# One weight block of the experts in the place of channel-major x, with x made anew from its token-major copy at the first scatter

## What is computed

```python
for l in range(DEPTH):
    xn = rms_norm(x, norm_mix[l])
    c_q, c_kv, k_rope, dq, dk, dv, mu, mv, mo, mg = jnp.split(xn @ w_in[l], split_at, axis=-1)
    ...
    x = x + jnp.concatenate([y_mla, y_dil, y_ml], axis=-1) @ w_out[l]
    x = x + hier_moe(rms_norm(x, norm_ffn[l]), ...)        # 16 experts
# hier_moe: h = silu(x @ w_gate) * (x @ w_up) * weight_of_token ; y = h @ w_down
```

## Time and profile before

| | |
|---|---|
| median of 3 runs | 1823.51 us (1822.35 to 1825.17) |
| the profiled execution | 1822.44 us |
| its span, first to last instruction | 1820.7 us |
| PE busy, of the span | 1776.5 us (98%) |
| DVE / ACT busy | 741.8 us (41%) / 309.2 us (17%) |
| moved by DMA | 546.86 MB, mean 300 GB/s |
| expert stage of layer 0 / layer 1, first expert product to the last scatter | about 462 to 915 us / 1367 to 1817 us |

### The profile page before, as it was taken

One profiled execution on the slowest core, in us unless ns is written; L12 is line 12 of the kernel. 1 busy time (PEld: TensorE's weight loads), 2 busy tenths in 40 slices (PEclk: granted clock), 3 DMA queues, 4 the chain that ended last, 5 costly groups with the idle time before them and its releaser, 6 DMA issues.

```text
span 1820.7 us, 27290 instructions
## 1 busy us (share of the span) xinstructions
PE 1776.5 (98%) x11754; PEld 1338.8 (74%) x11754; DVE 741.8 (41%) x1563; ACT 309.2 (17%) x830; POOL 13.8 (1%) x27
## 2 busy tenths in 40 slices
PE   9999999999999999899999999999999999999898
PEld 9788888899665566655597888878995755657555
DVE  3477665676302212012225775656762111121122
ACT  3023222211210020100021231222121200202000
POOL 1000000000000000000000000000000000000000
PEclk9999999999999999999999999999999999999999
DMA  9433443537999999999974342444479999999997
GB/s 386 155 150 125 165 168 133 197 143 282 364 427 428 426 427 427 427 428 422 414 292 150 134 174 115 168 170 160 189 283 372 429 426 428 426 429 426 427 422 300
DMA packets 52012, 546.86 MB, mean 300 GB/s; under 512 B 5936, under 2 KB 6064, under 8 KB 15664
## 3 DMA queue, kind: packets, MB, share of 16 engines
q1 hardware_dynamic: 49392, 531.47, 71.1%
q0 software_dynamic: 2496, 13.57, 2.0%
HBM read 540.78 MB, written 4.24 MB: 299 GB/s over the span
## 4 chain that ended last, share of the span: by engine, by line
PE 97%; issue 2%; DVE 1%; DMA 0%; SPq 0%; DVEq 0%
PE ps L872 94%; PE ps L926 1%; PE ps L1337 1%; PE ps L1230 0%; PE ps L942 0%; PE ps L934 0%; DMA ring<-in_w_lat 0%; DVE v_mla L2179 0%; PE ps L1354 0%; PE ps L1025 0%; DVE ring L1956 0%; PE ps L1111 0%; PE ps L1138 0%; DVE v_mla L2240 0%; DVE scr L1667 0%
## 5 line engine op out<-in xcount | busy, mean ns | idle before, releaser
L872 PE MATMUL ps<-ring,scr 128*64 128x256 f32 (+2 forms) x2176 | 439.3, 454 | 20.4 <-issue 20.3
L872 PEld LDWEIGHTS ps<-ring,scr 128*64 128x64 f32 (+1 forms) x2176 | 209.7, 141 | 190.9 <-issue 143.9
L872 PE MATMUL ps<-ring,XN 128*128 128x256 f32 (+2 forms) x1184 | 243.9, 363 | 1.0 <-DMA ring<-in_w_lat 1.0
L872 PEld LDWEIGHTS ps<-ring,XN 128*128 128x128 f32 x1184 | 212.4, 191 | 21.6 <-issue 2.1
L872 PE MATMUL ps<-ring,X 128*128 128x256 f32 x896 | 200.6, 379 | 0.0
L872 PE MATMUL ps<-XN,ring 128*128 128x128 f32 (+1 forms) x1312 | 195.8, 306 | 0.0
L872 PEld LDWEIGHTS ps<-XN,ring 128*128 128x128 f32 x1312 | 180.2, 191 | 12.7 <-issue 3.1
L872 PEld LDWEIGHTS ps<-ring,X 128*128 128x128 f32 x896 | 169.6, 190 | 22.7
L2240 DVE TENSOR_TENSOR v_mla<-scr,ps 128x256 f32<-128x256 f32 x32 | 13.5, 421 | 318.8 <-PE ps L872 318.8
L2192 DVE TENSOR_TENSOR X<-X,ps 128x512 f32<-128x512 f32 x128 | 88.0, 687 | 90.6 <-PE ps L872 89.9
L872 PE MATMUL ps<-PR,prob 128*128 128x256 f32 x512 | 120.7, 387 | 3.9 <-issue 3.9
(11 more groups left out here) (304 smaller groups left out, 2152.2 us busy)
## 6 DMA issues: line engine op xcount, KB each, us to landing
ring<-in_moe_w_gate SPq DMA_DIRECT2D x38, 2048.0 KB, 25.7
ring<-in_w_main SPq DMA_DIRECT2D x36, 2048.0 KB, 9.3
ring<-in_moe_w_down SPq DMA_DIRECT2D x32, 2048.0 KB, 30.6
ring<-in_moe_w_up SPq DMA_DIRECT2D x30, 2048.0 KB, 26.7
ring<-in_w_out_a SPq DMA_DIRECT2D x16, 1280.0 KB, 5.7
PR<-in_moe_w_up SPq DMA_DIRECT2D x10, 2048.0 KB, 28.0
XN<-in_moe_w_down SPq DMA_DIRECT2D x10, 2048.0 KB, 31.0
ring<-in_moe_w_up SPq DMA_DIRECT2D x20, 1024.0 KB, 25.8
```

What stands on the lines that cost most here:

```text
L872: return pe.matmul(o, lhsT, rhs, start=start, stop=stop, skip_group_check=True)
```

## The change

It does four things.

1. A tenth place, `IN_X`, is the memory of `X`. It is used once a layer: the block `g11_0` goes there, when `xt7` is made. SP issues it after the whole loads of pair 0 and ahead of the pieces. All blocks after it in the order move one place on in the ring.
2. One block fewer comes in pieces. During `g0_0` and `u0_0` come `dn10_0`, `dn11_0`, `g00_1`, `g01_1`; during `g1_0` only `u00_1`; during `u1_0` `u01_1` and `g10_1`. `dn01_0` is loaded whole, in `IN_XN`, before the first product. When `dy1_0` is done, `g11_1` and `u10_1` are issued, as before, and from there on the same blocks are freed at the same points of PE's program as before.
3. In the scatter of pair 0, each of the 8 pieces begins with 4 products of `xtok` tiles with the identity (128x128 results), which put x into the bank; `Y` times `Sw` is accumulated on top.
4. `add_moe` of pair 0 copies the bank to `X` where it added before.

```diff
+IN_XN, IN_PR, IN_BIAS, IN_X = NSLOT, NSLOT + 1, NSLOT + 2, NSLOT + 3
+EARLY = "g11_0"
...
-    for j, name in enumerate(EXPERT):
+    for j, name in enumerate(n for n in EXPERT if n != EARLY):
         r.once(name, experts[j % len(experts)])
+    r.once(EARLY, IN_X)
...
-IN_PIECES = {"dn01_0": "g0", "dn10_0": "g0", "dn11_0": "u0", "g00_1": "u0",
-             "g01_1": "g1", "u00_1": "g1", "u01_1": "u1", "g10_1": "u1"}
+IN_PIECES = {"dn10_0": "g0", "dn11_0": "g0", "g00_1": "u0", "g01_1": "u0", "u00_1": "g1", "u01_1": "u1", "g10_1": "u1"}
...
+            if SLOTS.where(name) == IN_X:
+                return ready(f"xt{TOKENS_LATE[-1]}", l)
...
                     if i == 0:
+                        load(EARLY, l, gate[l, 1, 1])
                         for q in range(4):
                             load_piece("g0", q)
...
                         pe.wait_ge(*freed(name, l))
+                        if i == 0:
+                            for q in range(2):
+                                for t in range(NT):
+                                    c = q * S + t * P
+                                    mm(bank(name)[:, c:c + P], xtok[:, t, (2 * k + q) * P:(2 * k + q + 1) * P], ident, q == 0 and t == 0, False)
                         for q in range(2):
-                            last = mm(bank(name)[:, q * S:(q + 1) * S], Y[:, (2 * k + q) * P:(2 * k + q + 1) * P], Sw)
+                            last = mm(bank(name)[:, q * S:(q + 1) * S], Y[:, (2 * k + q) * P:(2 * k + q + 1) * P], Sw, i > 0, True)
...
-                        dve.tensor_tensor(x, x, bank(name), ALU.add).then_inc(*read(name))
+                        if i == 0:
+                            dve.tensor_copy(x, bank(name)).then_inc(*read(name))
+                        else:
+                            dve.tensor_tensor(x, x, bank(name), ALU.add).then_inc(*read(name))
```

More of the change, by code:

```diff
@@ L349 @@
 EXPERT = [f"{n}{j}_{i}" for i in range(NE // 2) for n in ("g0", "u0", "g1", "u1", "dn0", "dn1") for j in range(2)]
-IN_XN, IN_PR, IN_BIAS = NSLOT, NSLOT + 1, NSLOT + 2
+IN_XN, IN_PR, IN_BIAS, IN_X = NSLOT, NSLOT + 1, NSLOT + 2, NSLOT + 3
+EARLY = "g11_0"
 SUMS_SLOT = 3
@@ L357, in plan_slots @@
 def plan_slots():
-    r = Uses(NSLOT + 3)
+    r = Uses(NSLOT + 4)
     r.part = "layer"
@@ L541, in build @@
         fbias = probf[0:H_D, 6 * S:8 * S]
-        spare = {IN_XN: xnf, IN_PR: prf[:, at + 1024:at + 1024 + SLOT],
+        spare = {IN_XN: xnf, IN_X: X[:, :, :].rearrange("p k s -> p (k s)"), IN_PR: prf[:, at + 1024:at + 1024 + SLOT],
                  IN_BIAS: BIAS[:, :, :].rearrange("p h n -> p (h n)")[:, 0:SLOT]}
@@ L566, in grow @@
             return probf[0:H_M, at:at + S]
-        slot_full = [sem(f"slot_full{s}") for s in range(NSLOT + 3)]
+        slot_full = [sem(f"slot_full{s}") for s in range(NSLOT + 4)]
         psum_full = [sem(f"psum_full{b}") for b in range(8)]
@@ L751, in _ @@
                 gate, up, down = a["moe_w_gate"], a["moe_w_up"], a["moe_w_down"]
-                source = {"dn01_0": down[l, 1, 0], "dn10_0": down[l, 0, 1], "dn11_0": down[l, 1, 1], "g00_1": gate[l, 2, 0],
-                          "g01_1": gate[l, 3, 0], "u00_1": up[l, 2, 0], "u01_1": up[l, 3, 0], "g10_1": gate[l, 2, 1]}
+                source = {"dn10_0": down[l, 0, 1], "dn11_0": down[l, 1, 1], "g00_1": gate[l, 2, 0], "g01_1": gate[l, 3, 0],
+                          "u00_1": up[l, 2, 0], "u01_1": up[l, 3, 0], "g10_1": gate[l, 2, 1]}
                 def load_piece(reader, q):
@@ L780, in _ @@
                             for j in range(2):
-                                if (n, half, i) != ("g", 0, 0) and f"{n}{half}{j}_{i}" not in IN_PIECES:
+                                if (n, half, i) != ("g", 0, 0) and f"{n}{half}{j}_{i}" not in IN_PIECES and f"{n}{half}{j}_{i}" != EARLY:
                                     load(f"{n}{half}{j}_{i}", l, w[l, 2 * i + j, half])
```

## The result

| | before | changed |
|---|---|---|
| median of 20 runs each, on the same chips | 1821.76 us | 1826.22 us |
| range of the runs | 1819.78 to 1826.44 | 1821.58 to 1829.73 |
| ratio, with 95% interval | | 1.0024 [1.0017, 1.0030] |
| the profiled execution, and its span | 1822.44, 1820.7 us | 1822.67, 1820.9 us |

The change makes the kernel slower by 0.24%, 4.4 us (3.1 to 5.5). The forecast was +3.2 us. The two profiled executions differ by only 0.2 us: single executions of one kernel scatter by several us, and this one of the changed kernel is the second fastest of its 20.

The account below looks back on a forecast made before the run. The DMA engines, through the landings of expert blocks, were taken as the bound. Lateness of 1.9 us in layer 0 and 1.3 us in layer 1 gave +3.2 us, a median of 1826.7 us; range 1819.5 to 1830.5.

Parts of the forecast that it names:

- likeliest case: Whole kernel: lead lost, block behind dy1_1 late in both layers; +1 to +3.6 us, chance 0.45.
- dear products: Scatter of pair 0: identity products at the dearest gather price, 8.7 us; +6.8 us, 1830.3 us, chance 0.34.
- half kept lead: Expert stages: half the early block's lead survives; 1819.5 us, set as the low end of the range.
- The early block: Start of the expert stage: g11_0 issued near 458.5 fills the DMA hole; lead at most 2.8 and 3.6 us.
- The products with the identity: Scatter of pair 0, in pair 1: 64 more instructions per layer cost PE 6.9 us, unhidden; ends 6.4 and 8.7.
- the dear end: Upper price of the 64 identity instructions per layer, from gathers in groups of 8: 8.7 us.
- second rival: Scatter of pair 0: the identity products cost more, 8.7 us; +6.8 us in all, chance 0.34.
- The delay and the queue: At dy1_1: issue 6.9 us later, 5.0 and 5.6 us of queue left; landings late by 1.9 and 1.3 us.
- the lead drops out: At dy1_1: the queue empties before the issue, block lands at issue + 8.0 us, however large the lead was.
- From there to the end: After dy1_1: PE's later waits shrink its delay to the landings' 1.9 and 1.3 us; layer 0 waits some 9 us.
- Moved places: Layer boundary: blocks sit one place on; c0 of layer 1 waits for g1_7, already read; costs nothing.
- The faster rival: Expert stages: identity products cost the stream nothing, both leads stay; -6.4 us, 1817.1 us; chance 0.13, wholly or by half.

Follow-up runs that it names:

- r1: The changed kernel run once more, nothing altered, on another chip: 1827.01 us, 1.0023 against the kernel before.
- e3: The kernel before plus only the identity products in pair 0's scatter and the copy, no early block: 1827.22 us, 1.0027.
- e7: The changed kernel with X's memory also used for a second block, u01_1; identity products still in pair 0's scatter: 1823.65 us, 1.0013.
- e8: The kernel before plus only the identity products, placed in pair 1's scatter (in pair 2), no early block: 1820.66 us, 0.9995.
- e2: The changed kernel with the identity products of pieces 4 to 7 moved one pair later, those of 0 to 3 left: 1818.57 us, 0.9984.
- e1: The changed kernel with all identity products moved from pair 0's scatter to pair 1's (in pair 2): 1815.22 us, 0.9958.
- r2: X's memory used for two blocks, identity products in pair 0's scatter, timed again beside the changed kernel: 1823.30 us, 1.0003.
- e9: The kernel before with only layer 1's load of c2 also waiting for layer 0's last down product, dy4_7: 1819.68 us, 0.9991.
- e6: The changed kernel with X's memory used for two blocks and the identity products in pair 2's scatter (in pair 3): 1810.96 us, 0.9937.

## Why the prediction was right

*The number.* +4.4 us was measured (3.1 to 5.5), +3.2 was forecast. That 1826.7 and 1826.22 us agree so well is luck in part: I started from a median of three, 1823.51 us, and the 20 runs put the kernel before at 1821.76. By its size +4.4 lies above my likeliest case (+1 to +3.6, just inside "no change") and in the band of the dear products; by its mechanism it is the likeliest case, with a price of 7.15 us, just where the loss passes 3.6 (2 x 7.1 - 5.0 - 5.6; I had written 7.2). The low end of my range, 1819.5, is 0.8 us under the half kept lead that I named for it (1823.5 - 3.2 = 1820.3).

*The early block.* Right: issued 0.3 us ahead of the first gather, hole filled. The lead at `dy1_0` was to be 2.8 and 3.6 us; by landings it was 2.8 (53.9 against 56.7 us behind the first gather) and 1.9 (55.7 against 57.6). Why the second is smaller this trace doesn't show; in r1 it is 4.0 us (53.6).

*The products with the identity.* I took 6.9 us; they cost 7.15, 8 of them 0.90 us from start to start (551.52 to 552.42). The slope from 16 to 32 gathers was nearly the price; the dear end, 8.7 us, is out, and with it the second rival's cause.

*The delay and the queue.* Right in mechanism and size: +2.0 and +1.4 us by landings against +1.9 and +1.3 forecast, and a block issued into an empty queue took 7.9 us in both layers. The Trainium skill, "DMA: Bandwidth & Descriptors", section "Anatomy of one DMA — SWDGE (gpsimd) path", gives about 2.0 us of fixed cost and 436 GB/s for a DMA on GpSimd's path. An estimate by it for this block is 6.8 us; on SP's queue the traces show 7.6 to 8.3 behind the dry places. That the lead drops out was the boldest step, and e3 (no lead) beside the changed kernel and e7 (larger lead) shows it by landings: 117.7, 117.6, 118.0 us in layer 0.

*From there to the end.* Forecast: PE's later waits take its delay down to the lateness of the landings. e8 shows it: no cost for 7.15 us of PE in pair 2. The sum of the later waits was to fall to some 9 us and fell to 11.6. I had left out that a wait can also cost clock: behind the last wait of layer 0 (2.29 us) 80 instructions took 12.47 us, with a granted clock of 0.71 and 0.86 in the two windows of 4 us, so partly at 1.2 GHz and not 2.4; the same group takes 10.78 us behind the wait of 0.70 us before. But in layer 1 it is the kernel before that pays, so the two nearly cancel, and r1 pays in neither layer. The chains of layer 1, before and changed:

```profile
1725.07 2.30 issue
1727.37 12.27 PE ps L872 x80
```

```profile
1727.41 0.60 issue
1728.01 10.78 PE ps L876 x80
```

By landings the loss is 3.4 us, by PE's arrival at the stage's end 3.8 (4.1 in r1), and by the medians 4.4, with 3.1 to 5.5 us in its interval. The last 1 us or less stays open; this clock cost doesn't explain it.

*Moved places.* Right for the changed kernel in that `c0` costs nothing: its first issue didn't come 2 us later, as I had said, but 1.2 us earlier (424.5 us behind the first gather, 425.7 before). But I had looked at `c0` alone. In the kernels with X used twice the rotation moves `c2`, and that is worth 0.9 to 2.0 us of pause at the boundary.

*The faster rival.* It turned, as priced, on the delay of PE in pair 1: e2 (3.6 us of delay) and e1 (none) stand on its side.

## What to carry to other kernels

Where transfers bound a stage, an early start is a lead in the queue, and it lasts only until the next place where the queue runs dry; look for the shallowest queue behind the place where the lead is made, and price what PE is delayed there, beyond the queue that is left, at its full time. Behind that place the same work was free here (e8), where the queue at the next refill was some 15 us deep (in the kernel before, the block issued at 611.06 us landed after 23.4 us). The time from issue to landing, less that into an empty queue, reads the depth straight from the trace. Work that an early load makes necessary belongs where that depth is largest: the same 64 matmul instructions turned a loss of 4.4 us into a gain of 7.6 (5.3 to 10.0) by standing one pair later.

## What was not expected of the hardware

- A pause of PE at the boundary of the layers, behind a branch, was 2.8 to 3.1 us in the eight traces in which `c2` doesn't wait (DMA share 1.03 and 0.97 in the two windows before it in the kernel before) and 1.2 to 2.3 us in the six in which it does (0.76 and 0.82 in r2, 0.70 and 0.89 in e9).
- After a pause of 3.06 us (r1) the granted clock was 0.57 in the next window, partly 1.2 GHz, and 8 instructions took 3.59 us instead of 1.97. After one of 3.04 us in the same kernel (changed) they took 1.97, and after one of 2.16 us (e6) 2.94. The length of the pause alone doesn't decide it.
- Single executions of one kernel start the first expert stage between 456.3 and 459.9 us (the changed kernel, twice profiled), with the same code ahead of it.
